# Expert outputs stored as rows of a table, and a ring of ten weight parts in the experts of a two-layer encoder

## The reference

```python
def moe_swiglu(h, w_router, w_gate, w_up, w_down):
    logits = (h @ w_router).astype(jnp.float32)
    top_val, top_idx = lax.top_k(logits, TOP_K)
    top_w = jax.nn.softmax(top_val, axis=-1)
    combine = jnp.sum(jax.nn.one_hot(top_idx, N_EXPERTS, dtype=jnp.float32) * top_w[..., None], axis=-2)
    out = jnp.zeros(h.shape, jnp.float32)
    for e in range(N_EXPERTS):
        y = swiglu(h, w_gate[e], w_up[e], w_down[e]).astype(jnp.float32)
        out = out + combine[..., e:e + 1] * y
    return out.astype(h.dtype)
```

## Time and profile before

| | us |
|---|---|
| median of 3 runs | 1599.41 (1598.8 to 1600.95) |
| the profiled execution, whole | 1598.67 |
| its span | 1596.9 |
| first matmul of expert 0 | 699.05 |
| first matmul of expert 1 | 807.26 |
| TensorE busy in the span | 1550.0 (97%) |
| granted clock, mean | 0.993 |

### The profile page before, as it was taken

One profiled execution on the slowest core, in us unless ns is written; L12 is line 12 of the kernel. 1 busy time (PEld: TensorE's weight loads), 2 busy tenths in 40 slices (PEclk: granted clock), 3 DMA queues, 4 the chain that ended last, 5 costly groups with the idle time before them and its releaser, 6 DMA issues.

```text
span 1596.9 us, 29275 instructions
## 1 busy us (share of the span) xinstructions
PE 1550.0 (97%) x12168; PEld 848.9 (53%) x12168; DVE 848.5 (53%) x1762; ACT 476.2 (30%) x699; POOL 58.3 (4%) x43
## 2 busy tenths in 40 slices
PE   6999999999999989999999999999999999999997
PEld 5877788888887877853433333333333333333332
DVE  5877676556687766744534345246245344443352
ACT  5577665444456966420000000000000000000001
POOL 0130000000003200010000000000000000000000
PEclk9999999999999999999999999999999999999998
DMA  9434365544443333559999999999999999999994
GB/s 385 152 145 149 115 226 189 205 184 184 185 172 132 136 155 108 199 197 416 399 384 425 408 386 410 404 386 420 395 402 416 371 423 415 382 414 412 384 409 188
DMA packets 66960, 473.78 MB, mean 297 GB/s; under 512 B 7408, under 2 KB 7664, under 8 KB 10768
## 3 DMA queue, kind: packets, MB, share of 16 engines
q1 hardware_dynamic: 64480, 460.88, 72.8%
q0 software_dynamic: 1920, 10.09, 1.8%
q10 hardware_dynamic: 432, 0.96, 0.2%
HBM read 469.80 MB, written 2.10 MB: 296 GB/s over the span
## 4 chain that ended last, share of the span: by engine, by line
PE 80%; DVE 9%; ACT 7%; issue 3%; DMA 1%; SPq 0%; DVEq 0%; ACTq 0%
PE bank L1298 26%; PE turn L1310 12%; PE mid L1298 10%; PE turn L1316 6%; PE bank L512 5%; PE bank L514 5%; PE bank L513 5%; DVE w_lo L507 2%; PE mid L512 2%; PE mid L514 2%; PE mid L513 2%; ACT w_hi L500 2%; DVE xT L1558 1%; DMA raw<-in_stream 1%; PE mid L1138 1%
## 5 line engine op out<-in xcount | busy, mean ns | idle before, releaser
L1298 PE MATMUL bank<-raw,gT 128*32 128x512 f32 (+1 forms) x4096 | 439.0, 566 | 0.7 <-ACT gT L957 0.7
L507 DVE TENSOR_TENSOR w_lo<-raw,w_hi 128x1024 fp32r<-128x1024 f32 x202 | 254.0, 1268 | 153.6 <-ACT w_hi L500 151.8
L1298 PEld LDWEIGHTS bank<-raw,gT 128*32 128x32 f32 x4096 | 135.4, 110 | 275.6 <-issue 266.4
L512 PE MATMUL bank<-w_hi,a_hi 128*128 128x512 f32 (+1 forms) x608 | 242.4, 399 | 15.2 <-DVE w_lo L507 12.0
L500 ACT ACTIVATE w_hi<-raw 128x1024 fp32r<-128x1024 f32 x202 | 211.2, 1056 | 127.3 <-PE bank L514 81.1
L514 PE MATMUL bank<-w_hi,a_lo 128*128 128x512 f32 (+1 forms) x608 | 234.9, 386 | 0.0
L513 PE MATMUL bank<-w_lo,a_hi 128*128 128x512 f32 (+1 forms) x608 | 234.6, 386 | 0.0
L1774 DVE STREAM_TRANSPOSE hT<-eh 32x128 f32<-32x128 f32 (+1 forms) x768 | 219.8, 286 | 24.2
L1310 PE MATMUL turn<-raw,hT 128*32 128x512 f32 x1792 | 213.1, 592 | 0.0
L1298 PE MATMUL mid<-raw,gT 128*32 128x256 f32 (+1 forms) x2048 | 189.0, 486 | 0.0
L983 ACT ACTIVATE eh<-bank 128x512 f32<-128x512 f32 (+1 forms) x32 | 17.4, 544 | 546.9 <-PE bank L1298 318.6
(11 more groups left out here) (240 smaller groups left out, 1323.7 us busy)
## 6 DMA issues: line engine op xcount, KB each, us to landing
raw<-in_stream SPq DMA_DIRECT2D x436, 1024.0 KB, 7.2
wg<-in_gates POOLq DMA_DIRECT2D x2, 2048.0 KB, 10.5
gain<-in_norms POOLq DMA_DIRECT2D x4, 512.0 KB, 4.1
x<-in_x SPq DMA_DIRECT2D x2, 512.0 KB, 6.5
raw<-in_stream SPq DMA_DIRECT2D x2, 512.0 KB, 6.5
tokens<-xs POOLq DMA_DIRECT2D x1, 1024.0 KB, 4.3
out_x<-xn SPq DMA_DIRECT2D x4, 256.0 KB, 2.2
const<-in_consts ACTq DMA_DIRECT2D x1, 752.0 KB, 11.6
```

Source lines behind the costliest of these rows:

```text
L507: nc.vector.tensor_tensor(w_lo[:, h % H, :], raw[:, part % R, lo:lo + HALF], w_hi[:, h % H, :].bitcast(F32), ALU.subtract).then_inc(lo_rea ...
L512: nc.tensor.matmul(out_, s_hi, wh, start=start, stop=False)
L1298: ins = nc.tensor.matmul(bank_[strip(s_), 0:w], gT[:, kt, strip(t_)], w_c, start=kt == 0, stop=kt == KT - 1)
```

## The change

Two things. First, for experts 0 to 6 of the first pass the steps with `y_hi`, `y_lo`, `selT` and `combine` are gone. ACT and DVE write the 96 x 1024 outputs into `y_rows` (three and one instructions), POOL stores them as 96 rows of a table in HBM behind its fetch of the same expert's turn, and when the rows of expert 6 are stored POOL reads, by four indirect DMAs, for each token the row of its first and of its second pick among experts 0 to 6 (row 0 of the table is zero). DVE finds row numbers and shares once, in expert 0 (`find_picks`, 22 small instructions), and adds the picked rows to x in expert 7, ahead of its last column group (`add_picked`). Expert 7's outputs go as before.

Second, the experts' parts run in a ring of ten: `wide` is laid over `raw`, `w_hi` and `w_lo`. The parts 0 to 5 are loaded in the static stage as before, 6 to 9 when the static stage's last product is done (`used` at `U0`), and every later one when the part ten ahead of it in the order is used. SP's loop over experts is written out. `wide` and `picked` lie over other tiles of the same memory; no tile of the old layout moves.

```diff
+WIDE = R + H
+def wide_ring():
+    loads = [(STATIC_PARTS + R - 1 - i) // R for i in range(R)] + [0] * (WIDE - R)
+    place, value = [], []
+    for m in range(EXPERTS * E_PARTS):
+        p = (STATIC_PARTS + m) % R if m < R else m if m < WIDE else place[m - WIDE]
+        loads[p] += 1
+        place.append(p)
+        value.append(16 * loads[p])
+    return place, value, loads
+PLACE, LANDED_AT, LOADS = wide_ring()
...
-        landed = [sem(f"part_landed{i}") for i in range(R)]
+        landed = [sem(f"part_landed{i}") for i in range(WIDE)]
...
         def part_landed(eng, pas, i, e):
+            if pas == 0:
+                m = e * E_PARTS + i
+                eng.wait_ge(landed[PLACE[m]], LANDED_AT[m])
...
-            expert_loads(U0)
+            for m in range(R, E_LAST):
+                sp.wait_ge(used, U0 if m < WIDE else U0 + m - WIDE + 1)
+                sp.dma_start(wide[:, PLACE[m], :], stream[STATIC_PARTS + m, :, :]).then_inc(landed[PLACE[m]], 16)
...
             pool.dma_start(tokens.rearrange("(b p) d -> p b d", p=P), xs[:, :, :]).then_inc(stored, 16)
+            nc.gpsimd.memset(y_rows[:, :], 0.0).then_inc(row_blank, 1)
+            pool.wait_ge(row_blank, 1)
+            pool.dma_start(table[0:1, :], y_rows[0:1, :]).then_inc(row_stored, 16)
             pool.wait_ge(stored, 16)
...
                 fetch(FETCHES[0], e)
+                pool.wait_ge(row_act, 3 * (e + 1))
+                pool.wait_ge(row_dve, e + 1)
+                pool.dma_start(table[1 + e * CAP:1 + (e + 1) * CAP, :], y_rows[0:CAP, :]).then_inc(row_stored, 16)
+            pool.wait_ge(row_stored, 16 * EXPERTS)
+            pool.wait_ge(pick_ready, 2 * TB)
+            for k in range(2):
+                for b in range(TB):
+                    nc.gpsimd.indirect_dma_start(picked[:, 2 * b + k, :], None, table,
+                                                 bass.IndirectOffsetOnAxis(ap=pick_i[:, k, b:b + 1], axis=0)
+                                                 ).then_inc(pick_landed[2 * b + k], 16)
...
+                def output_rows(e):
+                    act.wait_ge(used, u0 + e * E_PARTS)
+                    act.wait_ge(row_stored, 16 * e)
+                    nc.scalar.activation(y_rows[0:CAP, xslice(0)], turn[0][0:CAP, :], ACT.Copy).then_inc(row_act, 1)
+                    nc.scalar.activation(yt[0:2 * STRIP, :], turn[1][2 * STRIP:P, :], ACT.Copy).then_inc(row_act, 1)
+                    nc.scalar.activation(y_rows[2 * STRIP:CAP, xslice(1)], turn[0][CAP:P, :],
+                                         ACT.Copy).then_inc(row_act, 1)
...
-                            if i == at_ and not is_first(pas, e):
+                            if i == at_ and pas:
...
-                        w_ = raw[:, (STATIC_PARTS + i) % R, :]
+                        if pas == 0 and (e or i >= R):
+                            w_ = wide[:, PLACE[e * E_PARTS + i], :]
+                        else:
+                            w_ = raw[:, (STATIC_PARTS + i) % R, :]
...
-                            if i == N_IN and not is_first(pas, e):
+                            if i == N_IN and pas:
                                 pe.wait_ge(summed, 4 * y0 + 4 + e * 4)
+                            elif i == N_IN and e:
+                                pe.wait_ge(row_act, 3 * e)
+                                pe.wait_ge(row_dve, e)
...
+                def add_picked():
+                    for k in range(2):
+                        for b in range(TB):
+                            dve.wait_ge(pick_landed[2 * b + k], 16)
+                            if k:
+                                dve.wait_ge(picked_added, b + 1)
+                            nc.vector.scalar_tensor_tensor(
+                                out=x[:, b, :], in0=picked[:, 2 * b + k, :], scalar=pick[:, 2 + k, b:b + 1],
+                                in1=x[:, b, :], op0=ALU.mult, op1=ALU.add).then_inc(picked_added, 1)
...
+                    if pas == 0 and e:
+                        dve.wait_ge(row_act, 3 * e - 1)
+                        nc.vector.tensor_tensor(y_rows[0:2 * STRIP, xslice(1)], turn[1][0:2 * STRIP, :],
+                                                yt[0:2 * STRIP, :], ALU.add).then_inc(row_dve, 1)
...
+                    if is_first(pas, e):
+                        find_picks()
                     for q, w in enumerate(QUADS):
+                        if is_last(pas, e) and q == len(QUADS) - 1:
+                            add_picked()
```

More of the change, by code:

```diff
@@ L274, with build @@
 V_END = V_ROUTER + KT * EXPERTS
-def build(nc, stream, gates_w, x_in, norms, consts_in, vecs_in, out, tokens):
+def build(nc, stream, gates_w, x_in, norms, consts_in, vecs_in, out, tokens, table):
     with ExitStack() as ctx:
@@ L288, in build @@
         keep("front", [P, 480])
+        with ExitStack() as m:
+            wide = keep("wide", [P, WIDE, PART], into=m)
         raw = keep("raw", [P, R, PART])
@@ L310, in build @@
             att_lo = keep("att_lo", [P, 2, T], F32R, m)
+        with ExitStack() as m:
+            picked = keep("picked", [P, 2 * TB, D], into=m)
         keep("wg_place", [P, 4 * KT * P])
@@ L367, in build @@
             most_i = keep("most_i", [P, 2], I32, m)
+            code = keep("code", [P, 4, TB, EXPERTS - 1], into=m)
+            pick = keep("pick", [P, 4, TB], into=m)
+            pick_i = keep("pick_i", [P, 2, TB], I32, m)
+            y_rows = keep("y_rows", [P, D], into=m)
         bank = [ctx.enter_context(nc.psum_tensor(f"bank{i}", [P, CB], F32)) for i in range(4)]
@@ L471, in build @@
         summed = sem("output_added")
+        row_act = sem("output_rows_scalar_steps")
+        row_dve = sem("output_rows_vector_steps")
+        row_blank = sem("output_rows_blank")
+        row_stored = sem("output_rows_stored")
+        pick_s = sem("pick_steps")
+        pick_ready = sem("picks_ready")
+        pick_landed = [sem(f"pick_landed{i}") for i in range(2 * TB)]
+        picked_added = sem("picked_added")
         zeroed = sem("zeroed")
@@ L584, in outputs_from @@
         def outputs_from(pas):
-            return ROUNDS[pas] - (pas == 0)
+            return (-EXPERTS, 1, EXPERTS + 2)[pas]
         def turns_from(pas):
-            return E_TURNS * EXPERTS * pas + 4 * (pas - 1)
+            return E_TURNS * outputs_from(pas)
         def part_landed(eng, pas, i, e):
-            n = STATIC_PARTS + pas * E_LAST + i
-            eng.wait_ge(landed[n % R], 16 * (n // R + 1) + e * (16 * E_PARTS // R))
+            if pas == 0:
+                m = e * E_PARTS + i
+                eng.wait_ge(landed[PLACE[m]], LANDED_AT[m])
+            else:
+                p = (STATIC_PARTS + i) % R
+                eng.wait_ge(landed[p], 16 * (LOADS[p] + (pas - 1) * E_LAST // R + i // R + 1) + e * (16 * E_PARTS // R))
         block = ctx.enter_context(nc.Block())
@@ L647, in _ @@
                     for i in range(R):
-                        sp.wait_ge(used, U0 + pas * E_LAST - R + i + 1)
+                        sp.wait_ge(used, U0 + pas * E_LAST)
                         load((STATIC_PARTS + i) % R, STATIC_PARTS + i)
@@ L975, in experts @@
                         most_reg.append(act.value_load(most_i[0:1, 0:1], min_val=0, max_val=T))
-                    if not is_first(pas, e):
+                    if pas:
                         output(e)
+                    elif e:
+                        output_rows(e)
                     for q, w in enumerate(QUADS):
@@ L1264, in experts @@
                 if pas:
-                    pe.wait_ge(summed, 4 * c0)
+                    pe.wait_ge(summed, 4 * y0)
                 for j in range(2):
@@ L1708, in output, with step, find_picks @@
                                             y_hi[0:CAP, xslice(1)].bitcast(F32), ALU.subtract).then_inc(y_dve, 1)
+                def step(ins, n):
+                    ins.then_inc(pick_s, 1)
+                    dve.wait_ge(pick_s, n)
+                def find_picks():
+                    ok, val, hit, sh = (code[:, i, :, :] for i in range(4))
+                    first, rest, s_first, s_rest = (pick[:, i, :] for i in range(4))
+                    ranks_ = slot[:, :, 1:EXPERTS]
+                    for e in range(EXPERTS - 1):
+                        ins = nc.vector.tensor_scalar(val[:, :, e:e + 1], ranks_[:, :, e:e + 1], 1.0 + e * CAP, None,
+                                                      ALU.add)
+                        ins.then_inc(pick_s, 1)
+                    step(nc.vector.tensor_scalar(ok, ranks_, float(CAP), None, ALU.is_lt), EXPERTS)
+                    step(nc.vector.tensor_tensor(ok, ok, mask[:, :, 0:EXPERTS - 1], ALU.mult), EXPERTS + 1)
+                    step(nc.vector.tensor_tensor(val, val, ok, ALU.mult), EXPERTS + 2)
+                    step(nc.vector.tensor_tensor(sh, share[:, :, 1:EXPERTS], ok, ALU.mult), EXPERTS + 3)
+                    step(nc.vector.tensor_reduce(first, val, AX.X, ALU.max), EXPERTS + 4)
```

(21 more changed lines are left out.)

## The result

The changed kernel takes 1580.99 us (median of 4 runs, 1579.82 to 1582.91) against 1599.11 us before (4 runs); the ratio is 0.9884, 95% interval 0.9869 to 0.9899. That is 18.1 us, where 17.6 had been forecast (1581.8). The profiled execution takes 1579.82 us with a span of 1578.0.

A forecast was written before the change was run, and what follows sets the result against it. TensorE's matmuls were taken to set the pace, not the DMA engines. Profiled 1598.67 less 17.7 for the combines, all else nothing, gave 1581.0; with 0.74 for the runs' median 1581.7, stated as 1581.8 us; range 1579.8 to 1591.

The forecast's parts named there:

- The combines: Seven experts' combines, 56 matmuls, leave TensorE; on the path with nothing beside them, 17.7 us, the whole gain.
- ACT, DVE, add_picked, find_picks at nothing: Expert-start work, 4.8 us of row finding and 6.0 us of additions in expert 7 all fit in slack: no cost.
- POOL at nothing: POOL's added memset, one-row store, 7 stores and 4 indirect reads delay nothing; first fetch perhaps 3 us later, needed 67 after.
- The loads: Weight stream in the experts: demand 414 GB/s against supply of about 425, 2.6% of room, costed at nothing.
- a share of 1.00 isn't fullness: DMA engines' share in the experts is no measure of fullness: packets stretch when there is less to move.
- (b): Rival, chance 0.06: DMA engines are full now and additions cost their bytes, so no difference, 1596 us.
- (c): Rival, chance 0.04: full engines, and 11 new transfers each pay 2.1 us beyond bytes; slower, 1619 us.
- (a): Rival, chance 0.17: experts partly short of loads, POOL transfers costing 2.1 us beyond bytes; 1597 at worst, 1584 to 1594 at half.
- The reserve of ten parts: Loads needed nine parts after issue, 23.2 us, so landing may grow by 16 us before TensorE waits.
- 10 us or so: Sign of being right: the loads' landing time may rise to this; under 23 us it costs nothing.

The follow-up runs named there:

- ring10_combine: The kernel before with the ring of ten alone, the combines staying on TensorE: 1600.18 us, ratio 0.9999 to the kernel before.
- no_blank_ring6: The changed kernel with a ring of six and without the memset of `y_rows` (zero row stored from `y_hi`): 1582.39 us, ratio 0.9889 to the kernel before.
- no_rows: The changed kernel without row outputs of experts 0 to 6: no `y_rows`, stores, picks or additions; 1582.59 us, ratio 0.9891 to the kernel before.
- rows_ring6: The changed kernel with a ring of six in place of ten, memset kept: 1585.90 us, ratio 0.9906 to the kernel before.
- stores7: The changed kernel with each store of 96 rows made seven times, six into memory nobody reads: 1607.00 us, ratio 1.0045 to the kernel before.
- light_ring10: The changed kernel with the third matmul group left out in in parts of k tiles 4 to 7: 1561.86 us, ratio 0.9764 to the kernel before.
- light_ring6: The lighter TensorE of light_ring10 with a ring of six in place of ten: 1573.45 us, ratio 0.9835 to the kernel before.

## Why the prediction was right, step by step

**The combines, 7 x 2.53 = 17.7 us.** Right: 17.68 from gather to last down, and the period of 108.21 us is that of expert 0. ring10_combine (the ring without it: no gain) and no_blank_ring6 (the rows without the deeper ring: the whole gain) show that it is this and not the ring.

**ACT, DVE, add_picked, find_picks at nothing.** Right, shown together by no_rows. The sizes: `find_picks` runs from 704.35 to 707.9 us, 3.6 us instead of 4.8; `add_picked` takes 4.87 instead of 6.0:

```profile
1527.62 4.87 DVE L1816 SCALAR_TENSOR_TENSOR x<-picked,pick,x 128x1024 f32<-128x1024 f32 x4
```

DVE is done with the last group's `hT` at 1539.8 us, and TensorE reads it in the last two parts, from 1558.5 us on.

**POOL at nothing.** Right for this kernel by its timing alone. The text looked for who waits for POOL and found no one; it didn't ask whom the memset blocks. That the memset costs nothing is luck of the prediction: the cover is the late load of `gain`, behind the four parts sent ahead, and rows_ring6 shows the price if it is gone, 2.8 us.

**The loads.** The step was right in its outcome and mis-sized: supply is 419 GB/s, not 425, so the room is 1.0% instead of 2.6%. The 425 came from stretches without a fetch; the mean over whole experts, with the 0.7 to 0.9 us that a fetch costs beside its bytes, is what counts. That a share of 1.00 isn't fullness was right: the engines showed 1.00 at 401 GB/s and could give 419. Rivals (b) and (c) fall by that, and (a) and (c) also by their price: a store costs 1.0 us and not 0.9 + 2.1 (stores7), and a fetch 0.7 to 0.9 us beside its bytes and not 2.1 (light_ring10). The slow windows of the kernel before, 333 and 351 GB/s, both lie behind combines: ring10_combine still has 334 GB/s at the first place (1266 to 1276 us), and the changed kernel, without combines, has 422 at the second (1469 to 1479 us), though the picks are issued there. That SP issues late after a combine is the reading that fits; no run tests it by itself. The sum of rival (a) has two slips that this brings out: it keeps 1.2 us for the combines' gaps, which the change removes, and at half the price its own terms (7 x 0.56 + 5 + 4.2 = 13 us) stay under the 16 us of reserve, so that they give no wait and not 1584 to 1594.

The Trainium skill's figure of 358 GB/s ("DMA: Bandwidth & Descriptors", section "Where 436 GB/s comes from") is passed here as well. The Trainium skill's figure of about 425 GB/s for a core that streams alone ("HBM Reference", section "Specifications (TRN2)") agrees with the 422 measured.

**The reserve of ten parts.** Costed as harmless, and it is; but the gain doesn't need it. The picks lift the landing of the loads in expert 7 to 11 us (view of 1470 to 1500 us, changed kernel):

```profile
wide<-in_stream SPq DMA_DIRECT2D x12, 1024.0 KB, 11.3
picked<-table,pick_i POOLq DMA_INDIRECT x1, 16.8
```

A ring of six allows 12.9 us, which is why it gets by with four waits of at most 0.4 us that cost nothing. I had said 10 us or so.

## What to carry to other kernels

When two resources look full, take work off the one that the chain names, and measure how far the other is behind it: making the first lighter on purpose gives the second's own pace in one run (here 107.1 against 108.2 us). Read a supply over whole periods, not in the best stretch. A step that nobody waits for can still hold another engine while it runs: place a memset on POOL where DVE has nothing urgent, or reuse memory that is zero already.

## What was unexpected of the hardware

A memset of 0.97 us behind a DMA issue of 0.74 us on POOL stretched a DVE instruction of 0.17 us to 1.40 us; the 1.17 us in which TensorE stood for it were followed by a fall of the granted clock to a mean of 0.66 over 4 us (0.57 in light_ring6), and the gather took 1.6 us more. And a store of 96 rows of 4 KB on POOL's queue takes 1.0 us from a stream that is at its limit, of which 0.94 are its bytes, although it takes 7.7 us to land; an indirect fetch of as many rows takes 0.7 to 0.9 us beside its bytes.
